# More gate/value chunks of four feed-forward up stages as wide products, in a five-block transformer kernel on one Trainium2 core

## The reference, cut to what matters

```
def conv_gated_ffn(h, w_up, conv_w, conv_b, w_down):
    u = h @ w_up                      # 1024 -> 2 x 2752
    u = causal depthwise conv of width 3 over the tokens, + conv_b
    gate, val = jnp.split(u, 2, axis=-1)
    return (jax.nn.silu(gate) * val) @ w_down
```

## Time and profile before

| | us |
|---|---|
| runs of the kernel before (3) | 1476.39, 1476.89, 1477.18; median 1476.89 |
| the profiled execution's own time | 1478.02 |
| its span | 1476.0 |
| PE busy | 1468.6 |
| DVE busy | 1118.2 |
| ACT busy | 925.5 |
| POOL busy | 331.5 |

### The profile page before, as it was taken

The page is one execution under the profiler, slowest core; times in us unless marked ns, Lnnn a source line. Parts: engine busy times, 40 slices in busy tenths (PEclk is TensorE's granted clock), DMA queues, the critical chain, the costliest instruction groups (busy, mean ns, idle before and its releaser), DMA issues.

```text
span 1476.0 us, 26523 instructions
## 1 busy us (share of the span) xinstructions
PE 1468.6 (99%) x10440; PEld 1357.2 (92%) x10440; DVE 1118.2 (76%) x1885; ACT 925.5 (63%) x1536; POOL 331.5 (22%) x461
## 2 busy tenths in 40 slices
PE   9999999999999999999999999999999999999998
PEld 8999989899999898989989899999898999988888
DVE  7768898565578995787899566688995688798655
ACT  7776666456756664575676456766664558566453
POOL 2004222211132222212221221022212261022100
PEclk9999999999999999999999999999999999999999
DMA  7644656544345555562565545445655464355460
GB/s 276 199 159 139 225 200 219 169 163 164 115 136 209 202 201 196 180 193 85 201 204 197 198 161 196 159 138 206 206 194 198 159 215 172 114 200 205 176 224 32
DMA packets 39688, 265.03 MB, mean 180 GB/s; under 512 B 5248, under 2 KB 5563, under 8 KB 8977
## 3 DMA queue, kind: packets, MB, share of 16 engines
q1 hardware_dynamic: 36432, 255.54, 49.6%
q0 software_dynamic: 2992, 7.79, 2.2%
q10 hardware_dynamic: 144, 0.05, 0.0%
HBM read 262.24 MB, written 1.12 MB: 178 GB/s over the span
## 4 chain that ended last, share of the span: by engine, by line
PE 94%; DVE 3%; ACT 1%; DMA 1%; issue 1%; ACTq 0%
PE bank L1801 27%; PE bank L1798 14%; PE bank L1786 13%; PE bank L1787 12%; PE bank L1788 12%; PE bank L1849 6%; PE bank L1858 3%; PE bank L2032 1%; DVE w_lo L956 1%; DMA w_raw<-w_std 1%; PE bank L2021 1%; PE bank L2013 1%; PE bank L2012 1%; DVE tmp L1543 1%; PE bank L2385 1%
## 5 line engine op out<-in xcount | busy, mean ns | idle before, releaser
L956 DVE TENSOR_TENSOR w_lo<-w_raw,w_hi 128x2048 fp32r<-128x2048 f32 x239 | 549.6, 2307 | 74.4 <-ACT w_hi L411 74.3
L411 ACT CAST w_hi<-w_raw 128x2048 fp32r<-128x2048 f32 x239 | 452.8, 1903 | 83.6 <-DMA w_raw<-w_std 63.3
L1801 PE MATMUL bank<-h_both,w_hi 128*128 128x512 f32 x960 | 301.5, 395 | 0.0
L1786 PE MATMUL bank<-h_both,w_hi 128*128 128x256 f32 x992 | 284.6, 287 | 0.2 <-DVE w_lo L956 0.2
L1787 PE MATMUL bank<-h_both,w_hi 128*128 128x256 f32 x992 | 280.6, 283 | 0.0
L1788 PE MATMUL bank<-h_both,w_lo 128*128 128x256 f32 x992 | 280.5, 283 | 0.0
L1801 PE MATMUL bank<-act_both,w_hi 128*128 128x512 f32 x848 | 267.4, 395 | 0.0
L1798 PEld LDWEIGHTS bank<-h_both,w_lo 128*128 128x128 f32 x960 | 179.9, 188 | 43.7 <-DVE w_lo L956 1.6
L1786 PEld LDWEIGHTS bank<-h_both,w_hi 128*128 128x128 f32 x992 | 189.9, 191 | 5.4 <-issue 4.2
L1787 PEld LDWEIGHTS bank<-h_both,w_hi 128*128 128x128 f32 x992 | 190.0, 192 | 0.4
L1788 PEld LDWEIGHTS bank<-h_both,w_lo 128*128 128x128 f32 x992 | 190.0, 191 | 0.0
(11 more groups left out here) (236 smaller groups left out, 2547.7 us busy)
## 6 DMA issues: line engine op xcount, KB each, us to landing
w_raw<-w_std SPq DMA_DIRECT2D x239, 1024.0 KB, 4.9
act_both<-vec_dram POOLq DMA_DIRECT2D x56, 128.0 KB, 3.4
w_raw<-w_std SPq DMA_DIRECT2D x3, 512.0 KB, 8.4
x<-xT SPq DMA_DIRECT2D x2, 512.0 KB, 5.6
out<-x SPq DMA_DIRECT2D x3, 256.0 KB, 2.1
w_raw<-w_std SPq DMA_DIRECT2D x2, 256.0 KB, 4.7
par<-params SPq DMA_DIRECT2D x1, 446.0 KB, 6.8
cst<-consts SPq DMA_DIRECT2D x1, 256.0 KB, 9.3
```

The lines of the kernel that those rows point to most:

```text
L411: act.copy(w_hi[:, n % SLOTS, :], w_raw[:, n % RAW, :]).then_inc(hi_ready, 1)
L956: dve.tensor_tensor(w_lo[:, n % SLOTS, :], w_raw[:, n % RAW, :], w_hi[:, n % SLOTS, :].bitcast(F32), ALU.subtract).then_inc(lo_ready, 1)
L1786: pe.matmul(dst, wh, xh, start=first, stop=False, skip_group_check=shared)
L1801: done = pe.matmul(bank[:, :], weights[k][0], moving[k][1], start=False, stop=stop and k == len(weights) - 1, skip_group_check=True)
```

## The change

Chunks 3 to 9 and chunk 20 of the up stages of layers 0 to 3 are made as wide products, as chunks 10 to 19 are before. Everything that belongs to a wide chunk comes with it: ACT's two copies, DVE's two adds, the convolution out of `u_sb`. The leads of the weight splits and all other orders stay.

```
-WIDE_UP = (range(10, 20),) * 4 + (range(2, FT),)
+WIDE_UP = (range(3, FT - 1),) * 4 + (range(2, FT),)
```

## The result

The changed kernel takes 1496.69 us (median of 4 runs, 1496.22 to 1497.54) against 1477.04 before: 19.65 us more, a ratio of 1.0127 with a 95% interval of 1.0116 to 1.0139. The forecast was 1491.8, the range 1484 to 1499. The profiled execution has a span of 1495.0 us.

The account below looks back on a forecast made before the run. PE's matmul pace was taken to bound the kernel, with late DVE delaying each second down part: 3 x 3.51 + 4.42 = 14.95 us on a median of 1476.89 gave 1491.8 us, range 1484 to 1499.

Parts of the forecast that it names:

- DVE's lateness: Up stages: late DVE catches up 0.07 us a wide chunk instead of 1.66, staying late from chunk 5 to 20.
- PE's pace: Up stages: eight chunks a layer each 0.186 us quicker on PE, 5.95 us over four layers if nothing waits.
- Product 3: DVE's product of chunk 3 in layer 0 stays at 159.45, since its silu hangs on an unmoved transfer.
- Step 4: DVE's chunk 4 work, product to first tap, four taps and two splits: 7.70 us against 6.49 before.
- Steps: DVE's steps 5 to 20 in the up stage: 5.50 us each from product to product, 88.00 us in all.
- Step 21: DVE's last step of the up stage, untouched by the change: 3.98 us, putting product 21 at 259.13 in layer 0.
- The wait at chunk 7: Layer 0 up stage: PE waits 0.94 us for the first weight split made in DVE's step 4.
- The gap at the down stage: Layer 0, first down output: PE idles 3.78 us for weight chunk 23, split at the end of DVE's step 19.
- Tile 21: Second down part waits for ACT's copy: 3.51 us later in layers 0, 1 and 3, 4.42 in layer 2.
- Nothing is given back: Behind the second down part's start all queues shift alike, so the 3.51 us loss of layer 0 stays whole.
- rival 3: Clock falls to 1.2 GHz after PE's idle at the down stage: 6.5 us more, 1498.3 us, chance 0.10.
- Rival 4: DVE's first tap waits out POOL's subtraction: 0.29 us more in each of 17 steps, 1511.5 us, chance 0.03.

Follow-up runs that it names:

- e2: Kernel before with chunk 20 alone added to the wide ones, chunks 3 to 9 narrow: 1475.81 us, ratio 0.9985.
- e6: Kernel before with chunks 6 to 20 wide and ACT's lead of weight splits raised at step 6 in place of step 3: 1473.15 us, ratio 0.9968.
- e9: The changed kernel itself, run again unedited: 1497.86 us, ratio 1.0134 to the kernel before.
- e10: Changed kernel with 28 thrown-away matmuls ahead of the down stage in layers 0 to 3, second run of that kernel: 1492.18 us, ratio 1.0102.
- e8: Changed kernel with chunk 20 narrow again (3 to 19 wide): 1499.17 us, ratio 1.0144 to the kernel before.
- e7: Changed kernel with DVE's product of a wide chunk moved behind the two adds of the next wide chunk: 1501.91 us, ratio 1.0164.
- e4: Changed kernel with POOL's subtraction for the low part replaced by a shorter copy of the product, low parts wrong: 1476.76 us, ratio 1.000.
- e3: Kernel before with chunks 8 to 20 wide, 3 to 7 narrow: 1475.39 us, ratio 0.9982.
- e5: Changed kernel with ACT's lead of weight splits raised from 4 to 5 chunks at step 6 in place of step 3: 1494.27 us, ratio 1.0105.
- e11: Kernel before with chunks 5 to 20 wide and ACT's lead of weight splits raised at step 6 in place of step 3: 1475.71 us, ratio 0.9985.
- e1: Changed kernel with 28 thrown-away matmuls ahead of the down stage in layers 0 to 3, first run: 1495.18 us, ratio 1.0113.

## Why the prediction was right, and what it lacked

The sign and the place are as forecast. DVE's lateness, the mechanism of the forecast, gives two thirds of the loss (12.8 of 19.2 us in the stages); the other third is the fall of the clock, which the sum had at nothing. The size was 14.95 and measured 19.65 us. Point by point:

- PE's pace, 0.186 us a chunk: right (e2's stages 0.19 shorter, e6's 0.93 for five chunks).
- Product 3 unmoved: right (17.43 us behind chunk 3, before 17.60). Step 4: 7.71, forecast 7.70. Steps: 5.50, forecast 5.50. Step 5 of layer 0 was 5.84, since its silu waited for a transfer. Step 21: 3.96, forecast 3.98.
- The wait at chunk 7: 0.94 to 1.03 us between the starts, 0.7 to 0.8 more than the 0.23 of two matmuls at pace, forecast 0.94. The gap at the down stage: 4.04 us in layer 0 and 3.8 in the others, forecast 3.78.
- Tile 21 in layer 0: 260.23 + 4.17 = 264.40, 121.45 behind chunk 3 against 117.94: 3.51 us, forecast 3.51. In layers 1, 2 and 3 the same sum gives 3.22, 2.79 and 3.30. Layer 2 was forecast at 4.42: I took its late transfer for a property of the layer, and it didn't come again. Together 12.82 us in place of 14.95.
- "Nothing is given back": right, and nothing is lost further on.
- The step that failed is the clock, at nothing in the sum, priced as rival 3 and given a chance of 0.10. Its fall came in every layer and cost 19.22 - 12.82 = 6.4 us in the profile, 5.7 between e9 and e10; the rival's price was 6.5. The forecast stood on its own gap of 3.78 us, longer than any in the trace before, and took for the likelier case that the clock would hold. The earlier trace rows say that it holds through 1.17 us of idleness and nothing of longer ones. The Trainium skill ("TensorE: Matmul & The Clock Gate", part 1) has the clock fall by idleness, and here the traces agree: a mean clock of 0.84 to 0.89 behind gaps of 3.8 to 4.0 us. In e8 it stayed up behind one of 3.59. With the price of rival 3 in the sum the forecast would have been 1476.9 + 14.95 + 6.5 = 1498.3, 1.6 us too high, the error being layer 2.
- What was luck: two errors stood against each other. The clock took 6.4 us that the sum had at nothing, and the tile sums of the four layers came out 2.1 us shorter than forecast, 1.6 of it by layer 2's transfer. By DVE's lateness alone the time would have been near 1490. The steps were right to 0.01 us; the range was made for 0.1 us on them and for the clock case, and it is this width that takes in the measured time.
- Rival 4, the lock in full: steps stayed at 5.50, so out here. But in e7 a tap that met POOL's read at its very start lost 0.53 us of 0.75. How much a tap loses depends on where it meets the read.

Open: the reason why the clock falls behind one gap and not behind another nearly as long (e8). Not tried: keeping the low part of the product away from POOL altogether (on ACT, say), which would free DVE's tap with a right result. e4 only bounds it, at 5.31 us a step; its low parts are wrong.

## What to carry to other kernels

Ask of an edit that saves the bounding engine 3% what it does to the engine that feeds it: not to its mean load (DVE was at 76%), but to the rate at which it catches up from its latest point, here 1.66 us a chunk before and 0.07 after. Where lateness lasts to the end of a stage it comes out as one long wait of the bounding engine, and as here such a wait of TensorE can cost a second time, by the clock. A piece of the same edit, begun where the feeding engine has caught up, can win where the whole loses: e3 is 0.18% faster by the table alone, and e6, with ACT's lead moved too, 0.32%, where the full change is 1.27% slower.

## What the runs showed of the hardware

- A VectorE tap that reads two SBUF operands lasts 0.47 us alone, 0.77 when it starts 0.26 us into GpSimd's subtraction of 0.75 us, and 1.00 when it starts with it (e7). When it starts 0.52 us into it, it lasts 0.50 (before, chunk 19 of layer 0), and 0.13 us of overlap with a copy of one operand cost nothing (e4). A tap that reads the bank lasts 0.47 inside the subtraction too (before, layer 0, at 181.04).
- A weight split of 128x2048, both inputs in SBUF, lasts 2.28 us alone and 2.81 with a subtraction of 0.75 us in it (before, layer 0, at 249.54), 2.45 with a copy of 0.40 (e4, at 254.55). The delay goes the other way too: GpSimd's cast of 0.40 us lasts 0.58 when it starts inside a tap (e7, at 207.92).
- Gaps of 3.7 to 5.0 us between matmul starts came with a fall of the granted clock to 1.2 GHz in all 17 places where the profiles have them (four each in the two profiles of the changed kernel, e5 and e7, one in e8). Shorter ones weren't of one kind: it fell at 2.09 (e11, at 34.49), 2.34 and 3.57 (e8), 2.71 and 3.27 us (e1), and stayed up behind 2.01 and 3.59 (e8) and 2.87 (e10).
- Work that is thrown away can pay: 28 matmuls in each gap made the kernel 5.7 us faster.
